# Attention of a two-layer decoder kernel: another order of the work on all five engines

## The reference

```python
s = jnp.einsum('bnqkgd,bnjkd->bnkgqj', q, kb).astype(jnp.float32)
s = jnp.where(mask, s, -jnp.inf)
sink = sinks.astype(jnp.float32).reshape(1, 1, N_KV_HEADS, Q_PER_KV, 1, 1)
m = jnp.maximum(jnp.max(s, axis=-1, keepdims=True), sink)
e = jnp.exp(s - m)
pr = (e / (jnp.sum(e, axis=-1, keepdims=True) + jnp.exp(sink - m))).astype(vb.dtype)
o = jnp.einsum('bnkgqj,bnjkd->bnqkgd', pr, vb).reshape(B, S, N_Q_HEADS * HEAD_DIM)
return o @ w_o
```

## The kernel before, in words

| round | TensorE | VectorE | ScalarE |
|---|---|---|---|
| 0 | turn hn (s-2) | low row | high row, hnT |
| 1 | project(0,0) | | high v |
| 2 | weigh second half of s-1, project(1,0) | low v | out_hi (s-1, 1) |
| 3 | project(0,1) | out_lo (s-1, 1) | |
| 4 | project(1,1) | residual 0 | |
| 5 | logits (s-2) | residual 1 | |
| 6 | turn q, k (s+1); weigh first half of s | logits bias, kT, ms | square, qT |
| 7 | | tops of s+1, out_lo (s, 0), hn (s-1) | out_hi (s, 0) |

## Time and profile before

### The profile page before, as it was taken

The page is one execution under the profiler, slowest core; times in us unless marked ns, Lnnn a source line. Parts: engine busy times, 40 slices in busy tenths (PEclk is TensorE's granted clock), DMA queues, the critical chain, the costliest instruction groups (busy, mean ns, idle before and its releaser), DMA issues. The chain is left out here.

```text
span 5523.3 us, 92806 instructions
## 1 busy us (share of the span) xinstructions
PE 4774.7 (86%) x30609; PEld 3059.0 (55%) x31045; DVE 3030.8 (55%) x6066; ACT 1945.9 (35%) x2841; POOL 1557.1 (28%) x1159
## 2 busy tenths in 40 slices
PE   7928999999939999999488888855999999996998
PEld 7916776766724444444255555534666666663444
DVE  5664444444445555554477777764444444435665
ACT  6714433443321212121244444422444443323322
POOL 1114444443301111010133333313444444322332
PEclk9959999999969999999799999977999999998999
DMA  6739999989842222221455555527999999854443
GB/s 223 266 107 312 311 308 300 311 283 289 264 143 96 99 101 96 105 96 64 123 152 144 151 147 149 149 60 240 303 314 301 299 304 295 282 162 163 143 137 116
DMA packets 1012895, 1092.04 MB, mean 198 GB/s; under 512 B 709456, under 2 KB 720720, under 8 KB 1012816
## 3 DMA queue, kind: packets, MB, share of 16 engines
q1 hardware_dynamic: 966736, 923.26, 53.2%
q0 software_dynamic: 46080, 167.79, 9.1%
HBM read 695.58 MB, written 227.54 MB: 167 GB/s over the span
## 5 line engine op out<-in xcount | busy, mean ns | idle before, releaser
L724 POOL TENSOR_TENSOR ex_w_lo<-ex_raw,ex_w_hi 128x2048 bf16<-128x2048 f32 x192 | 779.2, 4087 | 1158.3 <-ACT ex_w_hi L778 1158.3
L778 ACT ACTIVATE ex_w_hi<-ex_raw 128x2048 bf16<-128x2048 f32 x384 | 707.3, 1900 | 525.1 <-PE ex_ps_y L110 188.7
L875 PE MATMUL ex_ps_gate<-ex_xT,ex_w_hi 128*128 128x0 bf16 x2048 | 570.6, 279 | 160.8 <-DMA ex_xT<-ex_xrow 127.6
L876 PE MATMUL ex_ps_gate<-ex_xT,ex_w_hi 128*128 128x0 bf16 x2048 | 570.3, 279 | 0.0
L877 PE MATMUL ex_ps_gate<-ex_xT,ex_w_lo 128*128 128x0 bf16 x2048 | 570.1, 279 | 0.0
L875 PE MATMUL ex_ps_up<-ex_xT,ex_w_hi 128*128 128x0 bf16 x2048 | 558.5, 273 | 0.0
L876 PE MATMUL ex_ps_up<-ex_xT,ex_w_hi 128*128 128x0 bf16 x2048 | 558.4, 273 | 0.0
L877 PE MATMUL ex_ps_up<-ex_xT,ex_w_lo 128*128 128x0 bf16 x2048 | 558.3, 273 | 0.0
L857 DVE COPY ex_y<-ex_ps_y 128x512 f32 x324 | 224.1, 692 | 566.9 <-PE ex_ps_y L110 510.4
L841 DVE TENSOR_TENSOR ex_aT<-ex_silu,ex_ps_up 128x384 bf16<-128x384 f32 x256 | 141.7, 554 | 714.6 <-PE ex_ps_up L877 528.3
L109 PE MATMUL ex_ps_y<-ex_w_lo,ex_aT 128*128 128x512 bf16 x1296 | 492.2, 380 | 8.8 <-DVE ex_y L857 0.3
(11 more groups left out here) (313 smaller groups left out, 9295.0 us busy)
## 6 DMA issues: line engine op xcount, KB each, us to landing
ex_raw<-in_w_exp_gate SPq DMA_DIRECT2D x128, 1024.0 KB, 11.3
ex_raw<-in_w_exp_up SPq DMA_DIRECT2D x128, 1024.0 KB, 13.9
ex_raw<-in_w_exp_down SPq DMA_DIRECT2D x128, 1024.0 KB, 5.9
y_rows<-ex_y SPq DMA_DIRECT2D x162, 512.0 KB
cb_hin<-h_mid SPq DMA_DIRECT2D x64, 512.0 KB, 4.2
mix_x<-in_x SPq DMA_DIRECT2D x32, 512.0 KB, 4.5
h_mid<-mix_h SPq DMA_DIRECT2D x32, 512.0 KB, 5.3
y_rows<-mix_zeros SPq DMA_DIRECT2D x32, 512.0 KB, 6.0
```

Of the source, the lines that this page charges most:

```text
L724: eng.tensor_tensor(w_lo[u][:, w], raw[:, c, :], w_hi[u][:, w], ALU.subtract).then_inc(lo_done, 1)
L778: act.activation(w_hi[u][:, c * WCHUNK:(c + 1) * WCHUNK], raw[:, c, :], ACT.Copy).then_inc(hi_done, 1)
L875: pe.matmul(out, hi, x_hi, start=j == 0, stop=False)
L876: pe.matmul(out, hi, x_lo, start=False, stop=False)
```

## The change

It keeps all the arithmetic and reorders it. Scores, maxima and exponentials run three pairs ahead instead of two. `qT` has two buffers. A new PSUM tile `ps_t` of two banks holds the turned q, the turned `hn` and the logits; the turned k shares a bank with the first weighing. In each round VectorE does `over(c+1)` first and `rests(c)` after it, then extra work, then `top(c+3)`. The extra work after the change:

| round | TensorE (after its scores) | VectorE | ScalarE |
|---|---|---|---|
| 0 | turn q, k (s+1); project(0,0) | ms (s-2) | qT |
| 1 | project(1,0) | hn (s-2) | high row |
| 2 | weigh second half of s-1 | | out_hi (s-1, 1), high v |
| 3 | turn hn (s-2) | out_lo (s-1, 1), low row | hnT |
| 4 | project(0,1) | kT, low v | |
| 5 | project(1,1), ahead of its scores | residual 0 | |
| 6 | weigh first half of s | residual 1 | out_hi (s, 0), square |
| 7 | logits (s-2) | out_lo (s, 0), logits bias | |

GpSimd's `rs` moves from round 7 to round 0 of the next step, behind `heads`. On SyncE's queue the rows go out in round 5 instead of 1, `kv_in` is loaded in round 5 instead of 3, `h4` goes out in round 7 instead of 6. The diff, cut to its core:

```diff
-        qT = m.sb("qT", [P, NP, P])
+        qT = [m.sb(f"qT{u}", [P, NP, P]) for u in (0, 1)]
-        ps_log, ps_k = ps_o[:, 0, 0:NLOG], ps_o[:, 1, 0:2 * P].rearrange("p (j n) -> p j n", j=2)
+        ps_t = m.ps("t", [P, D])
+        ps_log, ps_k = ps_t[:, 0:NLOG], ps_o[:, 0, 0:2 * P].rearrange("p (j n) -> p j n", j=2)
```

On GpSimd:

```diff
-                    if c == 7 and prev:
-                        pool.wait_ge(ms_done, s)
...
                     if c < NP - 1 and cur:
                         heads(s, c + 1)
                     if c == NP - 1 and nxt:
                         heads(s + 1, 0)
+                    if c == 0 and prev2:
+                        pool.wait_ge(ms_done, s - 1)
+                        wait(pool, hn_done, s - 2)
+                        pool.tensor_tensor(rs[:], ms[:], C.minus_half[:], ALU.pow).then_inc(rs_done, 1)
```

On ScalarE:

```diff
+                    if c < NP - 3 and cur:
+                        exps(s, c + 3)
+                    if c >= NP - 3 and nxt:
+                        exps(s + 1, c + 3 - NP)
```

On VectorE:

```diff
+                    if c < NP - 1 and cur:
+                        over(s, c + 1)
+                    if c == NP - 1 and nxt:
+                        over(s + 1, 0)
+                    if cur:
+                        rests(s, c)
...
-                    if cur:
-                        rests(s, c)
-                    if c < NP - 1 and cur:
-                        over(s, c + 1)
...
+                    if c < NP - 3 and cur:
+                        top(s, c + 3)
+                    if c >= NP - 3 and nxt:
+                        top(s + 1, c + 3 - NP)
```

On TensorE:

```diff
+                    if c < NP - 3 and cur:
+                        scores(s, u, c + 3)
+                    if c == 5 and prev:
+                        project(1, 1).then_inc(wo_mm, 1)
+                    if c >= NP - 3 and nxt:
+                        scores(s + 1, v, c + 3 - NP)
+                    if c == 0 and nxt:
                         t = s + 1
                         pe.wait_ge(q_ld[v], done(t, v))
                         pe.wait_ge(kv_ld[v], done(t, v))
-                        wait(pe, h4_done, 2 * s)
-                        wait(pe, ol_done, 2 * s)
+                        wait(pe, log_done, s - 2)
+                        wait(pe, ol_done, 2 * s - 1)
                         for k in range(KD):
-                            pe.transpose(ps_x[:, k * P:(k + 1) * P], q_in[v][:, k * P:(k + 1) * P], C.ident[:])
+                            pe.transpose(ps_t[:, k * P:(k + 1) * P], q_in[v][:, k * P:(k + 1) * P], C.ident[:])
...
+                    if c == 0 and prev:
+                        pe.wait_ge(ol_done, 2 * s - 1)
+                        wait(pe, h4_done, 2 * (s - 1))
+                        project(0, 0)
```

More of the change, by code:

```diff
@@ L1580, in step @@
                         act.activation(hrow[u][:, 0:D], hn[:], ACT.Copy).then_inc(hi_done, 1)
[L1581 to L1584, removed]
                     if c == 2 and prev:
                         out_hi(s - 1, 1)
-                    if c == 1 and cur:
+                    if c == 2 and cur:
                         act.wait_ge(kv_ld[u], done(s, u))
@@ L1661, in step @@
                 for c in range(NP):
+                    if c < NP - 1 and cur:
[4 more added lines that the diff above has]
+                        rests(s, c)
+                    if c == 0 and prev2:
+                        dve.wait_ge(ss_done, s - 1)
+                        dve.tensor_scalar(ms[:], ss[:], 1.0 / D, EPS, ALU.mult, ALU.add).then_inc(ms_done, 1)
+                    if c == 1 and prev2:
+                        dve.wait_ge(rs_done, s - 1)
+                        wait(dve, hnT_mm, s - 2)
+                        dve.scalar_tensor_tensor(out=hn[:], in0=h4[u][:], scalar=rs[:, 0:1], in1=g_ffn[:],
+                                                 op0=ALU.mult, op1=ALU.mult).then_inc(hn_done, 1)
                     if c == 3 and prev:
                         out_lo(s - 1, 1)
-                    if cur:
-                        rests(s, c)
-                    if c < NP - 1 and cur:
-                        over(s, c + 1)
[L1668 to L1679, removed]
+                    if c == 4 and nxt:
                         dve.wait_ge(turn_mm, s + 2)
@@ L1686, in step @@
                         last.then_inc(kT_done, 1)
[L1687 to L1697, removed]
+                    if c == 4 and cur:
+                        dve.wait_ge(vh_done, s + 1)
+                        vin = kv_in[u][:, KVW:2 * KVW].rearrange("p (j e) -> p j e", e=HEAD)
+                        dve.tensor_tensor(vp[u][:, 1, :, :], vin, vp[u][:, 0, :, :], ALU.subtract).then_inc(v_done, 1)
+                    if c == 3 and prev2:
                         dve.wait_ge(hi_done, s - 1)
@@ L1700, in step @@
                         dve.tensor_tensor(hrow[u][:, D:2 * D], hn[:], hrow[u][:, 0:D], ALU.subtract).then_inc(lo_done, 1)
+                    if c in (5, 6) and prev:
+                        residual(s - 1, v, c - 5)
+                    if c < NP - 3 and cur:
+                        top(s, c + 3)
+                    if c >= NP - 3 and nxt:
+                        top(s + 1, c + 3 - NP)
                     if c == 7 and cur:
                         out_lo(s, 0)
[L1703 to L1707, removed]
+                    if c == 7 and prev2:
+                        dve.wait_ge(log_mm, s - 1)
+                        at = slice(s - 2, s - 1) if isinstance(s, int) else bass.ds(s - 2, 1)
+                        dve.tensor_tensor(C.logits[:, at, :].rearrange("p a b -> p (a b)"), ps_log, bias[:],
+                                          ALU.add).then_inc(log_done, 1)
             steps(dve, step)
@@ L1766, in step @@
+                    if c == 3 and prev2:
                         pe.wait_ge(hn_done, s - 1)
-                        if cur:
-                            pe.wait_ge(qT_done, s + 1)
+                        if nxt:
+                            pe.wait_ge(qT_done, s + 2)
+                        else:
+                            wait(pe, log_done, s - 2)
                         for k in range(KD):
-                            mm = pe.transpose(ps_x[:, k * P:(k + 1) * P], hn[:, k * P:(k + 1) * P], C.ident[:])
+                            mm = pe.transpose(ps_t[:, k * P:(k + 1) * P], hn[:, k * P:(k + 1) * P], C.ident[:])
```

73 lines of the change are left out of this document (28 added, 45 removed).

## The result

Measured together, six runs of each: before 5531.09 us (5525.64 to 5535.33), after **5553.26 us** (5545.29 to 5555.73). The ratio is 1.0038, with an interval of 1.0025 to 1.0051: **slower by 0.38%**, 22 us. The forecast was 5532 us, no change; of its three chances, slower by more than 0.2% had the smallest, 0.25. The number lies inside the range of 5445 to 5562, but what happened is rival D. The profiled execution took 5554.3 us.

A forecast was written before the change was run, and what follows sets the result against it. No engine was full; waits filled the 29.87 us step beyond TensorE's 24.1. VectorE's 28.8 gave a 29.1 us step, plus 0.7 for clock: 29.8; 30 steps -2 us, first steps +1, so 5532 us, range 5445 to 5562.

The forecast's parts named there:

- rival D: Attention steps: clock low in every step from the turning of q through the quarters; 5553 to 5572 us, 15 in 100.
- The hold: GpSimd's `heads` holds up the second `rests` of each pair on VectorE: 0.82 us a round, 6.6 a step.
- Rival C: `rests` is not held on VectorE: a step of 25.5 us, up to 28; 5402 to 5475 us, 16 in 100.
- What the change takes away: Waits for exponentials (4.7 us a step) and for hn (2.76) go; if only this counted, 25.5 us a step.
- Costing the moved DMAs and kv_in's landing at nothing: DMAs of rows and kv_in move to round 5, that of h4 to round 7; assumed to cost nothing.
- VectorE's sum: VectorE's time a step: 22.6 us, less 0.4 for `nmx`, plus 6.6 for held `rests`, makes 28.8.
- The clock: TensorE's low clock expected again after the gap before the turning of q; 0.7 us a step, bounds 0 and 1.75.
- I take 0.7: Low clock's price in us a step, behind TensorE's gap before the turning of q; makes the step 29.8 us.
- The bound of 1.75: Upper bound in us a step for the low clock: half of 3.5 us at the low level.
- if over 30.5, look at the clock first: Sign for a held `rests` with a step over 30.5 us: check the clock, then the landing of kv_in.
- +1 expected: Steps 0 and 1 of the stage: the held `rests` has less to hide in, 1 us more.
- the clock stays high: Rival: `rests` held, but TensorE's gap breaks up; 29.1 us a step, 5495 to 5510 us, 16 in 100.

The follow-up runs named there:

- the other banks: The kernel after, with the logits moved to the projection's second bank so the turning of q no longer waits for their addition: 5498.35 us, 0.9935 of before.
- `rests` first: The kernel after, with rests(c) put in front of over(c+1) again and all else kept: 5397.18 us, 0.9750 of before.

## Why the prediction missed

- **The hold: right.** Place (second `rests` of each pair, in every round), cause and nearly the size: 0.77 us a pair (1.64 - 0.87) against 0.82. Rival C is refuted, and the one row of `rs` against two `rests` had pointed the right way.
- **What the change takes away: right.** The waits for the exponentials and for `hn` are gone, and the chain without the hold is 25.0 to 25.3 us where 25.5 was worked out. Costing the moved DMAs and kv_in's landing at nothing held: no wait for them is among those of the loop.
- **VectorE's sum: 1.5 us too high.** 28.8 us were summed up; 27.3 were measured, and the step with a high clock is 28.0, not 29.1. The hold was 0.4 a step smaller (eight times 0.05), `hn` 0.1 shorter (1273 ns against 1350). The rest is a fault of counting: the 22.6 I started from is the union of busy rows, where the tail of about 0.08 us of an operation counts only if nothing follows at once. In the two steps of the earlier trace rows VectorE had 42 idle pieces, in two of after 26; the tails of the 8 fewer per step lie under the next operation, 0.6 us. About 0.4 us stay unexplained.
- **The clock: the step that failed.** "I take 0.7" for the step should have been 2.7 us (30.72 - 28.02). The bound of 1.75, too, was too low. It was half of the low stretch of before, 3.5 us; after's is 6.8 us long, 5.4 of them with work under them, and half of 5.4 is 2.7. That the length would carry over was assumed and not shown by any row. So was the share, three steps in four, read in a kernel whose steps differ; in after all steps are alike and all fall. The text had named both ("all on the chain to scores 5", "in every step" in D) and yet the sum took less than before's cost per low step, 1.3. Why the stretch is 3.4 us in some kernels and steps and 6.8 in others stays open.
- **Rival D: right in kind, near in number by luck.** The clock is low in every step behind the gap, as D says, though it is back up before the first of the two quarters is done, where D had it low "through the quarters". D's own price, up to 2.0 us, was too low as well. With the real 2.7 on the summed 29.1 its time would have been some 5590 us; 5553.26 lies at the very edge of its 5553 to 5572 because VectorE's sum was 1.1 us too high. And the lower edge doesn't follow from D's 1.75: that gives 0.98 us a step and 5562 us.
- **The total.** The loop is 0.92 us a step above the forecast, 25 us in 27 steps: 2.0 too little for the clock, 1.1 too much for VectorE. The two errors point in opposite directions, so 5532 looks better than its working was. The sign that the text itself had set, "if over 30.5, look at the clock first", pointed to the right place. Outside the loop +1.4 us in the stage, against +1 expected, and 4.9 us beyond the stage, where nothing is changed; the runs of one kernel differ by 10 us among themselves.
- **The chances.** D got 15 in 100 and "the clock stays high" 16, though the first was the better supported: a gap as long as that of before, in front of a chain. Against D stood "the gap is no longer than before's", which is an argument for the same clock cost in each fall, not for fewer falls.

## What to carry to other kernels

Where GpSimd and VectorE both work in SBUF, give GpSimd its signal so that VectorE's next operations read PSUM: here the order of two operations was worth 2.9%. When a reorder gathers TensorE's idle time in one piece, don't take over the price of the low clock from another gap: both the length of the low stretch and the work under it can change. Here all that work was on the chain, and half of its time was lost in every step. A few idle matmuls in the gap are a quick test, and were here a gain (1.4%) by themselves. Before adding terms to an engine's busy time, check whether its idle pieces go as well, because their tails go with them.

## What the runs showed of the hardware that was not expected

- **No length of gap tells by itself whether the clock falls.** It fell in every step behind 2.5 to 2.6 us (after) and behind 1.39 us (the other banks), in five steps of 27 behind 1.0 to 1.6 us (`rests` first), and behind none of the gaps of 1.0 to 1.44 us that came after five idle matmuls; the one step of that kernel that fell did so behind 0.74 us in front of them. In before it fell behind 2.76 to 2.84 us in 20 steps of 27 and stayed up in seven, as behind the 2.76 us of the earlier trace rows. The comparison of 1.39 with 1.44 us suggests that what TensorE did before the gap counts along with it, but no run changes that alone. The Trainium skill (TensorE: Matmul & The Clock Gate, the section on a second failure mode) warns of swings from small idle pieces between groups of matmuls; the two kernels with gaps of 1.0 and 1.39 us agree. Why steps with the same gap and the same work part ways isn't settled by these runs.
- **The low stretch came in two lengths.** It was 3.4 to 3.5 us in before, in `rests` first and in half of the steps with the other banks, and 6.8 us in every step of after and in the other half of those steps. Its price depends on how much of it lies under work on the chain: 1.7 us where it was 3.4 long (`rests` first, 27.0 against 25.3) and 2.7 where it was 6.8 (after).
- **Useless work can be free and even pay.** 11 matmuls of 128x512 in each step, 2.5 us of TensorE, made the kernel 1.4% faster than after: VectorE sets the step (27.2 of 28.0 us busy) and the clock stays up.
- **GpSimd also comes in between two operations of VectorE that are queued back to back**, as one row of before had let expect: 8 times a step, some 0.77 us each time. A GpSimd operation on a column (`rs`, 0.55 us, at 3064.03) that starts under VectorE's maximum, which reads PSUM (at 3063.79), shows no delay.
